# A hybrid block on one Trainium2 core: S5 input matrices turned in four transposes, and stacked by stores to HBM and block loads

## The reference

```
xg = xf.reshape(bsz, s, S5_GROUPS, S5_GROUP)        # 64 groups of 16 channels
bb_re = coef_re[..., None] * br - coef_im[..., None] * bi
bb_im = coef_re[..., None] * bi + coef_im[..., None] * br
bu_re = jnp.einsum('bsgi,gpi->bsgp', xg, bb_re)      # 64 states for each group
bu_im = jnp.einsum('bsgi,gpi->bsgp', xg, bb_im)
_, _, h_re, h_im = lax.associative_scan(complex_linear_combine, (a_re, a_im, bu_re, bu_im), axis=1)
y = jnp.einsum('bsgp,gip->bsgi', h_re, c_re) - jnp.einsum('bsgp,gip->bsgi', h_im, c_im)
```

## Time and profile before

| | us |
|---|---|
| median of 3 executions (2100.47 to 2101.54) | 2100.74 |
| the profiled execution's own time | 2100.62 |
| its span in the trace | 2098.9 |
| PE busy | 2068.0 (99% of the span) |
| DVE busy | 1267.7 (60%) |
| ACT busy | 805.0 (38%) |
| POOL busy | 745.1 (36%) |

### The profile page before, as it was taken

The page is one execution under the profiler, slowest core; times in us unless marked ns, Lnnn a source line. Parts: engine busy times, 40 slices in busy tenths (PEclk is TensorE's granted clock), DMA queues, the critical chain, the costliest instruction groups (busy, mean ns, idle before and its releaser), DMA issues.

```text
span 2098.9 us, 30735 instructions
## 1 busy us (share of the span) xinstructions
PE 2068.0 (99%) x12124; PEld 1691.9 (81%) x12124; DVE 1267.7 (60%) x1779; ACT 805.0 (38%) x1055; POOL 745.1 (36%) x555
## 2 busy tenths in 40 slices
PE   7999999999999999999999999999999999999998
PEld 6798888887787787877878778777778888888886
DVE  6554343449789597895968959676433435454333
ACT  5433232354443544435444353453242222222223
POOL 0000000028576485764857648567201000100000
PEclk9999999999999999999999999999999999999999
DMA  8244343443333433334333343343356565553334
GB/s 257 62 127 130 104 130 90 116 129 95 109 104 104 113 102 107 104 105 113 104 105 105 105 111 104 105 116 102 105 166 206 171 187 151 177 150 111 113 122 149
DMA packets 382913, 260.63 MB, mean 124 GB/s; under 512 B 23769, under 2 KB 351810, under 8 KB 382146
## 3 DMA queue, kind: packets, MB, share of 16 engines
q1 hardware_dynamic: 364146, 203.16, 35.5%
q0 software_dynamic: 11408, 43.00, 6.1%
q10 hardware_dynamic: 7232, 12.72, 1.6%
HBM read 223.17 MB, written 27.28 MB: 119 GB/s over the span
## 4 chain that ended last, share of the span: by engine, by line
PE 91%; DVE 3%; DMA 2%; ACT 2%; issue 1%; POOLq 0%; ACTq 0%; DVEq 0%; SPq 0%
PE bank L456 29%; PE bank L458 28%; PE bank L457 27%; PE bank L1097 1%; DMA raw<-in_w_kv_mem_dram 1%; DVE wl L450 1%; PE bank L991 1%; PE bank L979 1%; DMA yst<-s_out 1%; ACT wh L442 0%; DVE lb L2042 0%; PE bank L1046 0%; PE bank L1035 0%; PE bank L1060 0%; PE bank L1067 0%
## 5 line engine op out<-in xcount | busy, mean ns | idle before, releaser
L456 PE MATMUL bank<-uh,wh 128*128 128x512 f32 x2048 | 825.9, 403 | 3.3 <-DVE wl L450 3.1
L458 PE MATMUL bank<-uh,wl 128*128 128x512 f32 x2048 | 799.2, 390 | 0.0
L457 PE MATMUL bank<-ul,wh 128*128 128x512 f32 x2048 | 799.0, 390 | 0.0
L450 DVE TENSOR_TENSOR wl<-raw,wh 128x1024 fp32r<-128x1024 f32 x352 | 468.5, 1333 | 477.6 <-ACT wh L442 476.1
L442 ACT ACTIVATE wh<-raw 128x1024 fp32r<-128x1024 f32 x352 | 370.5, 1058 | 554.5 <-DMA raw<-in_w_in_dram 184.2
L456 PEld LDWEIGHTS bank<-uh,wh 128*128 128x128 f32 x2048 | 384.7, 188 | 90.8 <-issue 10.2
L458 PEld LDWEIGHTS bank<-uh,wl 128*128 128x128 f32 x2048 | 384.4, 188 | 83.3
L457 PEld LDWEIGHTS bank<-ul,wh 128*128 128x128 f32 x2048 | 385.2, 188 | 74.1 <-issue 1.9
L622 POOL DMA_DIRECT2D gated_c<-ox x8 | 4.4, 544 | 375.3 <-DVE ox L1805 374.6
L663 POOL TENSOR_TENSOR hr<-tcos,gr 128x512 f32<-128x512 f32 x32 | 51.7, 1617 | 199.4 <-DVE gi L2135 199.2
L1449 ACT ACTIVATE gk<-bank 128x512 f32<-128x512 f32 x48 | 28.7, 599 | 190.7 <-PE bank L458 190.6
(11 more groups left out here) (355 smaller groups left out, 2827.0 us busy)
## 6 DMA issues: line engine op xcount, KB each, us to landing
raw<-in_w_in_dram SPq DMA_DIRECT2D x224, 512.0 KB, 3.9
raw<-in_w_kv_mem_dram SPq DMA_DIRECT2D x32, 512.0 KB, 4.0
raw<-in_w_out_dram SPq DMA_DIRECT2D x32, 512.0 KB, 3.6
gates<-gk ACTq DMA_DIRECT2D x48, 256.0 KB, 4.3
gates<-gates POOLq DMA_DIRECT2D x24, 512.0 KB, 4.6
raw<-in_s_w_glu_dram SPq DMA_DIRECT2D x16, 512.0 KB, 4.0
raw<-in_w_br_c_dram SPq DMA_DIRECT2D x16, 512.0 KB, 3.9
raw<-in_w_br_a_dram SPq DMA_DIRECT2D x16, 512.0 KB, 3.9
```

Of the source, the lines that this page charges most:

```text
L450: dve.tensor_tensor(k.wl[slot][:, c], k.raw[slot][:, c], k.wh[slot][:, c].bitcast(F32), ALU.subtract).then_inc(k.w_lo, 1)
L456: pe.matmul(o, ah, bh, start=start, stop=False)
L457: pe.matmul(o, ah, bl, start=False, stop=False)
L458: return pe.matmul(o, al, bh, start=False, stop=stop)
```

## The change

B is built and turned without its quarters: `bpad` shrinks to a fourth, and PE turns it in 2 transposes, into the free half of bank 5, beside the 2 of C. This PE step moves from after `until(12)` to after `until(9)` and `chunk_output(l, 3)`. ACT writes the high half `bsh`, DVE the low half `bsl`. SP stores `xbh`, `xbl`, `bsh` and `bsl` whole to two scratch tensors in HBM (4 stores), waits for the stores to land, and loads each quarter of `x4` and of `bs` with one load of 32 rows (8 loads). SP's loads of block 3 come behind all that, as they came behind the 16 copies.

```
@@ SP
     def input_rows(j):
+        wait_apart(k, sp, k.xb_l, count(j, 1, 1))
+        for n, half in enumerate((k.xbh, k.xbl)):
+            sp.dma_start(k.xb_d[n], half[:, :].bitcast(F32)).then_inc(k.x4_in, 16)
+        wait_apart(k, sp, k.bs_l, count(j, 1, 1))
+        for n, half in enumerate((k.bsh, k.bsl)):
+            sp.dma_start(k.bs_d[n], half[:, :, :].bitcast(F32).rearrange("p n c -> p (n c)")).then_inc(k.bs_in, 16)
         wait_apart(k, sp, k.yp, count(j, 0, 1))
-        wait_apart(k, sp, k.xb_l, count(j, 1, 1))
-        for r, half in enumerate((k.xbh, k.xbh, k.xbl, k.xbl)):
-            for q in range(4):
-                sp.dma_start(k.x4[32 * r:32 * r + 32, q, :].bitcast(F32), half[32 * q:32 * q + 32, :].bitcast(F32)).then_inc(k.x4_in, 16)
+        wait_apart(k, sp, k.x4_in, count(j, 32, 96))
+        for r in range(4):
+            sp.dma_start(k.x4[32 * r:32 * r + 32, :, :].bitcast(F32), k.xb_d[r // 2].rearrange("(q p) c -> p q c", q=4)).then_inc(k.x4_in, 16)
+        wait_apart(k, sp, k.bs_in, count(j, 32, 96))
+        for r in range(4):
+            sp.dma_start(k.bs[32 * r:32 * r + 32, :, :, :].bitcast(F32).rearrange("p q n c -> p q (n c)"),
+                         k.bs_d[r % 2].rearrange("(q p) c -> p q c", q=4)).then_inc(k.bs_in, 16)
@@ PE
     def s5_matrices(j):
         pe.wait_ge(k.s5_w, count(j, 13, 13))
-        pe.wait_ge(k.bp_l, count(j, 2, 2))
-        wait(pe, k.mod, count(j, 0, 32))
         wait(pe, k.ysum, count(j, 0, 1))
         for n in range(2):
-            for q in range(4):
-                pe.transpose(ps[3 + n][:, q * P:(q + 1) * P], k.bpad[:, n, q].rearrange("p r g i -> p (r g i)"), ident)
+            pe.transpose(ps[5][:, (2 + n) * P:(3 + n) * P], k.bpad[:, n].rearrange("p q g i -> p (q g i)"), ident)
@@ PE s5_inputs
-        pe.wait_ge(k.bc_s, count(j, 2, 3))
-        pe.wait_ge(k.x4_in, count(j, 256, 256))
+        pe.wait_ge(k.bs_in, count(j, 96, 96))
+        pe.wait_ge(k.x4_in, count(j, 96, 96))
@@ PE mixer
         until(9)
         if l: chunk_output(l, 3)
+        if j: s5_matrices(j)
         until(10)
         if j: keys_keys(j)
-        until(12)
-        if j: s5_matrices(j)
         until(13)
@@ ACT
-    def input_halves(j):
-        act.wait_ge(k.s5_w, count(j, 9, 13))
-        wait(act, k.s5_tr, count(j, 0, 1))
-        rows = k.bpad[:, :, :, :, :, :].rearrange("p n q r g i -> p (n q) r (g i)")
-        act.activation(rows[:, :, 2, :].bitcast(F32R), rows[:, :, 0, :], ACT.Copy).then_inc(k.bp_h, 1)
     def s5_matrices(j):
         act.wait_ge(k.s5_tr, count(j, 1, 1))
-        wait(act, k.bu, count(j, 0, 4))
-        for n in range(2):
-            act.activation(k.bs[:, n, :, :], ps[3 + n][:, :].rearrange("p (q c) -> p q c", q=4), ACT.Copy).then_inc(k.bc_s, 1)
+        act.activation(k.bsh[:, :, :], ps[5][:, 2 * P:4 * P].rearrange("p (n c) -> p n c", n=2), ACT.Copy).then_inc(k.bc_s, 1)
@@ ACT mixer
         if l: new_values(l, 2); new_values(l, 3)
-        if j: input_halves(j)
+        if j: s5_matrices(j)
         if l: output_squares(l)
         end_of(0)
-        if j: row_decays(j); decays(j); s5_matrices(j)
+        if j: row_decays(j); decays(j)
@@ DVE
     def input_halves(j):
-        dve.wait_ge(k.bp_h, count(j, 1, 1))
-        rows = k.bpad[:, :, :, :, :, :].rearrange("p n q r g i -> p (n q) r (g i)")
-        raw, high = (rows[:, :, r:r + 1, :].to_broadcast([P, 8, 2, 2 * GS]) for r in (0, 2))
-        tt(rows[:, :, 1:4:2, :], raw, high, ALU.subtract).then_inc(k.bp_l, 1)
-        dve.wait_ge(k.bp_l, count(j, 1, 2))
-        dve.tensor_copy(rows[:, :, 0, :], rows[:, :, 2, :]).then_inc(k.bp_l, 1)
+        dve.wait_ge(k.bc_s, count(j, 2, 2))
+        tt(k.bsl[:, :, :], ps[5][:, 2 * P:4 * P].rearrange("p (n c) -> p n c", n=2), k.bsh[:, :, :].bitcast(F32),
+           ALU.subtract).then_inc(k.bs_l, 1)
```

More of the change, by code:

```diff
@@ L130, in build @@
         k.rows_d = nc.dram_tensor("decay_rows", [HEADS, NT, P], F32, kind="Internal").ap()
+        k.xb_d = nc.dram_tensor("s5_inputs", [2, P, S], F32, kind="Internal").ap()
+        k.bs_d = nc.dram_tensor("s5_turned", [2, P, 2 * P], F32, kind="Internal").ap()
         k.zb_d = nc.dram_tensor("z_b", [W, S], F32, kind="Internal").ap()
@@ L214, in build @@
             k.craw = sb(area, "craw", [2, NS])
-            k.bpad = sb(area, "bpad", [2, 4, 4, 2, GS])
+            k.bpad = sb(area, "bpad", [2, 4, 2, GS])
+            k.bsh = sb(area, "bsh", [2, P], F32R)
+            k.bsl = sb(area, "bsl", [2, P], F32R)
             k.rq = sb(area, "rq", [S])
@@ L243, in build @@
             k.cpad = sb(area, "cpad", [2, 2, NS])
-            k.bs = sb(area, "bs", [2, 4, P], F32R)
+            k.bs = sb(area, "bs", [4, 2, P], F32R)
             k.bc = sb(area, "bc", [2, P])
@@ L335, in build @@
             sems("s5_in", "s5_w", "s5_tr", "bc_s", "args", "tab")
-        k.bp_h, k.bp_l, k.xb_l, k.x4_in = \
-            sems("bp_h", "bp_l", "xb_l", "x4_in")
+        k.bs_l, k.bs_in, k.xb_l, k.x4_in = \
+            sems("bs_l", "bs_in", "xb_l", "x4_in")
         k.bu, k.mod, k.dem, k.yp, k.ysum, k.y_st = \
@@ L627, in pool_program @@
         pool.memset(t[:, 0:3], 0.0).then_inc(k.pad_zero, 1)
-    pool.memset(k.bpad[:, :, :, :, :, :], 0.0).then_inc(k.pad_zero, 1)
+    pool.memset(k.bpad[:, :, :, :, :], 0.0).then_inc(k.pad_zero, 1)
     def mixer(j, l):
@@ L1082, in s5_inputs @@
     def s5_inputs(j, q):
-        pe.wait_ge(k.bc_s, count(j, 2, 3))
-        pe.wait_ge(k.x4_in, count(j, 256, 256))
+        pe.wait_ge(k.bs_in, count(j, 96, 96))
+        pe.wait_ge(k.x4_in, count(j, 96, 96))
         wait(pe, k.mod, count(j, 8 * q - 2, 32))
-        pe.matmul(ps[3][:, :], k.bs[:, 0, q, :], k.x4[:, q, :], start=True, stop=True)
-        pe.matmul(ps[4][:, :], k.bs[:, 1, q, :], k.x4[:, q, :], start=True, stop=True).then_inc(k.bu, 1)
+        pe.matmul(ps[3][:, :], k.bs[:, q, 0, :], k.x4[:, q, :], start=True, stop=True)
+        pe.matmul(ps[4][:, :], k.bs[:, q, 1, :], k.x4[:, q, :], start=True, stop=True).then_inc(k.bu, 1)
     def s5_outputs(j):
-        pe.wait_ge(k.bc_s, count(j, 3, 3))
+        pe.wait_ge(k.bc_s, count(j, 2, 2))
         pe.wait_ge(k.dem, count(j, 24, 24))
@@ L1943, in s5_matrices @@
                 r = slice(64 * g, 64 * g + 64)
-                tt(k.bpad[r, n, :, 0, g, :], k.bt[r, 2 * n, :, :], k.bt[r, 2 * n + 1, :, :], op).then_inc(w, 1)
+                tt(k.bpad[r, n, :, g, :], k.bt[r, 2 * n, :, :], k.bt[r, 2 * n + 1, :, :], op).then_inc(w, 1)
         for n, names in enumerate((("even", "odd"), ("neven", "nodd"))):
@@ L2125, in s5_states @@
         if part and q == 0:
-            dve.wait_ge(k.x4_in, count(j, 256, 256))
+            dve.wait_ge(k.x4_in, count(j, 96, 96))
         g, x1, x2, op = (gi, im, re, ALU.subtract) if part else (gr, re, im, ALU.add)
```

## The result

| | median us | range | runs |
|---|---|---|---|
| before, same chip | 2100.47 | 2098.92 to 2101.54 | 5 |
| after | 2106.99 | 2104.66 to 2109.90 | 5 |

The ratio is 1.0035, 95% interval 1.0024 to 1.0046: slower by about 0.35%. The forecast was 2105.5 us. The profiled execution of after took 2104.66 us, its span is 2103.0 us, and it was the fastest of the five, so its waits may be on the low side. In after's listing the three big matmuls are L460 to L462, the block loads L534 (x) and L537 (`bs`), `s5_inputs` is L1097 and L1098, and `bpad` is turned at L1087.

The account below looks back on a forecast made before the run. PE was taken to bound the kernel, busy 99% of the span. The terms -5.3 + 0.2 + 7 x 1.1 + 2.3 = +4.9 us on 2100.6 gave 2105.5 us, range 2095.0 to 2111.5.

Parts of the forecast that it names:

- What PE is relieved of: PE's transposes in each small pass: six fewer at 0.11 us each, 0.66 us in 8 passes, gain 5.3 us.
- SP and the transfers: Block loads complete after PE reaches L1087, its first `s5_inputs`: PE waits 1.1 us in seven passes, 2.3 in the first.
- The moved PE step: The transposes, moved earlier, wait for `cpad` about 0.2 us once, in the first pass; no wait in later passes.
- ACT and DVE: DVE's work behind the moved transposes comes some 1.3 us later, absorbed by idle time on DVE and POOL: cost nothing.
- rival 1: No wait at L1087, PE's first `s5_inputs`: 32-row loads run at 42 engine-us per MB, 2095.5 us; chance 0.16.
- Full sharing: Block loads at 84 engine-us per MB take 8.2 us; waits 1.9 and 3.1 us, 2111.9 us; chance with beyond 0.10.
- Late weights of block 3: Block 3's weights reach PE late, needing to land some 7 us after the forecast's time; chance under 0.01.

Follow-up runs that it names:

- two eighths: PE's first `s5_inputs` of a pass moved two eighths later, `until(18)` for `until(16)`, against after: 2099.65 us, ratio 1.0001 to before.
- after's repeat: The changed kernel run again unaltered, as base of the experiments: 2106.06 us, ratio 1.0031 to before.
- the kernel with more bytes: After plus four 64 KB loads per pass, half of `bs` again into a scratch tile, which PE's wait includes: 2120.71 us, ratio 1.0103 to before.
- the six transposes at the wait: After plus six transposes of the identity directly ahead of PE's wait for `bs`: 2107.05 us, ratio 1.0032 to before.

## Why the prediction was right, step by step

**What PE is relieved of** (-5.3): right. 0.65 us a pass by the six transposes put back (taken 0.66), 5.3 by the spans. In after the gaps fell by 4.4 and those behind them by 0.6, against -5.3 + 0.2 = -5.1 with the moved step's first pass.

**SP and the transfers** (+10.0): the right mechanism, with 11.3 measured. The stores of x took 5.4 us from first issue to landing (taken: 5.4). The loads ran at 76 engine-us per MB, where I had put 75 between the copies' 66 and the doubled 84. From the first load to PE's start it took 604.13 - 594.38 = 9.75 us, taken 9.1. The issues were faster than thought, 0.44 us in place of 0.63 each, and it made no difference, as the rate and not the issues bound. The first pass paid 2.1 (taken 2.3). The others paid 1.3 on the mean (taken 1.1), but from 0.4 to 2.3: "seven times 1.1" was right only as a sum.

The Trainium skill ("SBUF — State Buffer", section "Door 1: The DMA port swizzle") gives about 218 GB/s for 32 adjacent partitions. This trace agrees: 221 GB/s with all engines busy, and 340 when 128 partitions were written. The estimate that the prediction worked out from that figure, 7.2 us and a wait of 0.9, was a little too low here, as the prediction's own was.

**The moved PE step** (+0.2): right. PE waits 0.2 us for `cpad` in the first pass; four of the changed kernels list it.

**ACT and DVE** ("Cost: nothing"): right for seven passes. In the seventh, PE waits 1.7 us for DVE's `st`, in every kernel with the changed code, and 0.2 in before. The timelines of the sixth and the seventh pass of after, same lines, DVE and POOL:

```profile
1110.43 0.61 DVE L1938 TENSOR_TENSOR bt<-braw,s5h 128x64 f32<-128x64 f32 x4
1110.87 1.32 POOL L660 TENSOR_TENSOR farg<-farg,karg 128x512 f32<-128x512 f32 x1
1111.08 2.27 DVE L1944 TENSOR_TENSOR bpad<-bt 64x64 f32<-64x64 f32 x4
...
1113.38 0.79 DVE L1947 TENSOR_SCALAR cpad<-craw,cst 128x64 f32<-128x64 f32 x4
1113.99 1.32 POOL L664 TENSOR_TENSOR farg<-farg,karg 128x512 f32<-128x512 f32 x1
```

```profile
1241.03 0.35 DVE L2092 SCALAR_TENSOR_TENSOR st<-st,er,bank 128x128 f32<-128x128 f32 x1 [1.85 <-PE bank L1075]
...
1241.96 1.72 DVE L1938 TENSOR_TENSOR bt<-braw,s5h 128x64 f32<-128x64 f32 x4
1242.17 1.29 POOL L660 TENSOR_TENSOR farg<-farg,karg 128x512 f32<-128x512 f32 x1
1243.71 1.35 DVE L1944 TENSOR_TENSOR bpad<-bt 64x64 f32<-64x64 f32 x4
1245.10 2.14 DVE L1947 TENSOR_SCALAR cpad<-craw,cst 128x64 f32<-128x64 f32 x4
1245.21 1.28 POOL L664 TENSOR_TENSOR farg<-farg,karg 128x512 f32<-128x512 f32 x1
1247.15 0.33 DVE L2092 SCALAR_TENSOR_TENSOR st<-st,er,bank 128x128 f32<-128x128 f32 x1
```

Single operations of these groups that last over 1 us end with an operation of POOL. In the sixth pass there is one, the first for `bpad`: it starts 0.21 us after POOL's L660 does, and ends 0.08 us after that one's end, 1.20 us long in place of the 0.24 of the second. POOL's L664 starts when DVE's `cpad` operations are all but through. In the seventh pass DVE is later against POOL, and there are two: the third for `bt`, 1.32 us in place of 0.21, ends 0.09 us after L660, and the second for `cpad`, 1.27 us in place of 0.44, ends 0.05 us after L664. The first costs little more than the `bpad` operation in the other passes, and the `bpad` group is 0.9 us shorter for it; the second is new. In sum DVE is through with `cpad` 1.8 us later after PE's last matmul ahead of `st` than in the sixth pass. Before's seventh pass is like after's sixth (0.61, 2.27 and 0.80 us for the three groups). This pattern, an operation of DVE that ends with L660 in the other passes and with L660 and L664 in the seventh, is in all 13 traces of the changed code.

So DVE meets a second operation of POOL because it comes late: its first `st` starts 0.46 us after PE's last matmul has ended, against 0.11 in the other passes and in before, while POOL keeps its distance to PE. What holds `st` up for these 0.35 us stays open, and no edit here was aimed at it. The link from the late `st` to the second meeting with POOL is read from the timelines, not tested. Both are in every changed kernel, whatever its waits for `bs`, so they go with the changed code and not with the waits; a cost of this kind the prediction put at nothing. It is why the kernels without a wait for `bs` (2097.7 to 2099.7) stay above the 2095.5 us of rival 1. The rest of that distance is the last pass (waits for `dl` and `wl` that before has too, 1.4 and 1.6, of which the first grows by up to 0.4) and, with two eighths, more waits for `wl`.

**What was left out.** A wait of 2 us can cost more than itself, by the clock. The sum also missed the opposite: lateness at one point is given back at the next wait, here 3.3 us in the last pass. With the 1.5 us of the seventh pass these nearly cancelled in the profiled execution, and so the forecast's 2105.5 lies within 1.5 us of both medians (2106.99 and 2106.06) with 1.3 us too little of wait in it. The chain of transfers was read rightly; that the sum came so close is in part luck.

**The rivals.** No wait: fell with the write to 128 partitions, since its condition (a slow read side) isn't met. Full sharing, 84: the rate is 76, nearer to it than to the copies' 66, as assumed. Late weights of block 3: in after no wait of PE for `wl` is left behind the first 35 us.

## What to carry to other kernels

Work taken from the busiest engine pays only if what replaces it is there in time: read from the timeline when the engine comes to the first use and add up the whole chain of the new transfers up to it (stores landing, then bytes at the rate of their shape, then the fixed part). A transfer's rate goes by the partitions it writes, 76 against 46 engine-us per MB here with the same bytes and source. Where such a chain is a microsecond or two late, look first for a use that can stand a little later and a store that can go a little earlier; together they turned +6.5 us into -1.9. Early stores alone, in either order, saved 4.8 us; a second queue saved nothing. And when work moves on one engine, look at what a second one does at that moment: by the timelines, 0.35 us of lateness on DVE cost PE 1.5 us, as DVE ran into one more operation of POOL.

## What the runs showed of the hardware

PE's clock fell after some of the waits for `bs`. The last pass of after, in the view of windows of 1 us (after the busy time of each engine: PE's granted clock, DMA share, GB/s):

```profile
1395.00:1396.00 1.00, 0.40 (x1) 0.32 (x2) 1.00 (x1) 0.99 (x2) 1.00 (x2) 0.91 1.19 289
1396.00:1397.00 1.00, 1.00 (x4) 0.79 (x3) 1.00 (x1) 0.97 (x3) 1.00 (x1) 0.50 1.20 290
1397.00:1398.00 1.00, 1.00 (x4) 0.81 (x3) 0.96 (x2) 0.98 (x3) 0.60 (x2) 0.50 1.00 242
1398.00:1399.00 1.00, 1.00 (x3) 0.72 (x3) 0.96 (x2) 1.00 (x1) 1.00 (x2) 0.50 0.04 10
1399.00:1400.00 1.00, 1.00 (x5) 0.87 (x4) 0.42 (x1) 0.83 (x2) 1.00 (x2) 0.88 0.00 0
```

PE had stood idle for 1.79 us, and ran for about 3.4 us at the lower of its two levels (1.2 in place of 2.4 GHz), some eight matmuls at 0.43 us: +1.6 us. Of the waits for `bs` of 1.79 us and more, it fell around those of 1.79 us (after), 2.03 and 2.62 (after's repeat), 2.19, 2.87 and 3.12 (the kernel with more bytes), and did not around 1.83 (after), 2.02 (the six transposes at the wait), 2.07, 2.08, 2.13 and 2.41 (more bytes). The kernels with two queues are as mixed: it fell at 1.81, 1.83, 2.13, 2.23 and 2.49 us and not at 1.80 and 2.60. So the same wait costs 1.6 us more or not. Whether this is what spreads after's executions over 5 us and before's over 2.6 isn't shown: the granted clocks of after's five (0.996 to 0.998) don't go with their times.

The DVE operation on `bt`, `bpad` or `cpad` that started 0.06 to 0.21 us after POOL's TENSOR_TENSOR on `farg` (L660, L664 in after) ended 0.05 to 0.09 us after it and took 1.2 to 1.3 us, where its neighbours take 0.2 to 0.4. That is so in each of the seven later passes, in before and in the 13 traces of the changed code. It does not hold for every pair of operations: in the sixth pass of after the `bt` operations beside POOL's TENSOR_SCALAR L658 kept their 0.21 us, and `st`, which reads a bank, kept its 0.33 us beside L664.

Landing times follow what else is in flight: the same 256 KB store of `s_out` by POOL took 3.0, 4.9 or 7.3 us from issue to landing, and the same 128 KB stores of `bsh` and `bsl` by SP 1.7 to 6.0 (medians by kernel).
